# A down projection in Strassen's form: another order of its fourteen units, and of the work on the other engines around them

## The chip, the cores and the metric

The kernel runs on one NeuronCore of a Trainium2 chip. The metric is the device time of one execution in microseconds, as the median of several runs. The engines are called TensorE (matrix products), VectorE, ScalarE, GpSimd (almost unused here) and SyncE, whose queue issues all transfers from device memory.

## The reference, cut to what matters

The program runs two transformer blocks on 256 tokens of width 2048 in fp32. Each block ends with a feed-forward part with a hidden width of 5632. All that the change touches is the last product of these two parts and the work that runs beside it.

```python
# first block (D_MODEL = 2048, FFN_HIDDEN = 5632)
def swiglu(h, w_gate_up, w_down):
    gu = jnp.einsum('bsd,df->bsf', h, w_gate_up)
    gate, up = jnp.split(gu, [FFN_HIDDEN], axis=-1)
    return jnp.einsum('bsf,fd->bsd', jax.nn.silu(gate) * up, w_down)
...
h = h + swiglu(rmsnorm(h, ffn_norm_w[l]), w_gate_up[l], w_down[l])
```

After the first block stand its final norm and the pre-mix norm of the second block, so the tokens are squared, summed and multiplied by gains twice before the second block's first projections read them. The second block's feed-forward multiplies a depthwise convolution and gelu of the gate half with the up half, then multiplies by its own w_down, norms the result (post_ffn_gain) and adds it to the residual.

## The kernel before

**Units.** All weights stream through the core once, in units of 128 x 2048 fp32 (1 MB), in one fixed order. Each unit passes four steps. SyncE loads it into one of four slots of `raw`. ScalarE copies it, rounded to the TensorE format, to `w_hi` (`split`, line 737, semaphore `hi_made`). VectorE writes the remainder `raw - w_hi` to `w_lo` (`split`, line 1288, `lo_made`). TensorE multiplies with the high part (`hi_used`), then with the low part (`lo_used`). Activations are also kept as a high and a low half. `w_hi` and `w_lo` have two buffers each (SPLIT = 2), so the copy of unit u+2 waits until TensorE has read the high part of unit u, and its remainder until the low part is read. Each engine's instructions run in the order in which they are written; the loops over units on ScalarE and VectorE call `split(u + form + 2)` in each step and place their other work before or after it.

**Feed-forward stages.** Each feed-forward part has two groups. A group first computes 22 tiles of hidden values, two units for each (`gated`), and then multiplies them with its share of w_down (`down`). Of a pair of units, VectorE adds the accumulator halves (`total`, line 1300, which also frees the accumulator banks), scales them, and after ScalarE's activation multiplies gate and up; ScalarE copies the result (line 934 in the first, 1211 in the second feed-forward), and VectorE forms its remainder. Of the second feed-forward's last group, ScalarE then loads another function table (`prepare(ACT.Sqrt)`, line 752).

**The down projection.** It runs in two passes, p = 0 (the first) and 1 (the second), of two blocks of 512 output columns each. Of the 22 hidden tiles, the first eight are taken as a 2 x 2 block problem (two k-blocks of four tiles, two column blocks, two blocks of 128 tokens), which Strassen's scheme computes with seven block products instead of eight. A pass has 14 units, called forms: seven products M_1 to M_7 (12 matmuls each: `product`, lines 2338, 2340, 2344) and seven ordinary ones (24 matmuls each: PLAIN_1 to PLAIN_6, `by_tokens`, lines 2319 and 2326, and MIXED, `both_columns`, lines 2369 and 2377, which takes the last two tiles for both column blocks).

The products need sums of weight blocks. VectorE makes four in each pass (`weight_sum(u, n)`, line 1571, 128 x 2048 each):

- sum 1, `B_12 - B_11` into `w_sum`, is the weight of M_5; it waits for both pieces to be loaded
- sum 2, `B_22 - w_sum`, is that of M_6; it can only be made after M_5's remainder, because it overwrites `w_sum`
- sum 3, `B_22 - B_12` in B_12's slot, is that of M_7
- sum 4, `B_21 - w_sum` in B_21's slot, is that of M_4

`WEIGHT_SUMS` makes ScalarE wait for the sum instead of a transfer. The B pieces are loaded once and used for more than one form (`PIECE_OF`), so a pass loads 11 pieces. `PIECES` gives their order, the place in the slot order that each takes, and their content; `FREED_BY[n]` is the form whose remainder must be made before piece n may be loaded; `NEXT_SLOTS` is the slot order that the pass hands on. The first four pieces of a pass wait for the remainders of the four units before it, one each.

Products that feed more than one output block are read out of the accumulator while it goes on: `snap` on VectorE, or `first_out` on ScalarE in the second feed-forward's first group, counted by `snapped`. When a column block is complete, VectorE adds it to the tokens (`added`, line 1529) or to `ff_out` (`out_part`, `out_sum_both`), and frees the two banks.

**Token work behind the last down projection of the first block (g = 1).** For each block n of 512 columns: ScalarE squares the tokens (`v_square`, line 959); TensorE transposes them (`turn_tokens`, eight transposes, line 2434); ScalarE copies them with a gain to `xa`, the next projection's input (`both_high`, line 879, four instructions); VectorE makes the remainders (`tokens_low`, line 1537, four instructions, `op_lo`) and multiplies the tokens by a gain (`final_gain`, line 1667, two instructions, `h_read`); ScalarE squares these (`x_square`, line 966, two squares, each waiting for one of the two gains). Blocks 0 and 2 are handled at the end of the first and of the second pass, block 1 in the middle of the second pass, block 3 after the passes. The next projection (`first_two`, line 2293) takes its first 12 matmuls from blocks 0 to 2 and waits for `op_lo` of each tile.

## Time and profile before

| | |
|---|---|
| median of 3 runs | 2660.02 us (2659.88 to 2660.03) |
| the profiled execution | 2660.03 us, of which its instructions span 2658.2 us |
| TensorE busy | 2637.8 us, 99% of the span, 13950 matmuls |
| VectorE busy | 1854.8 us, 70% |
| ScalarE busy | 1303.6 us, 49% |
| GpSimd busy | 3.5 us |
| transfers | 497.23 MB, 53% of the queues' capacity in time |
| chain of work that ended last | TensorE 92%, VectorE 4%, transfers 2%, ScalarE 1% |
| mean granted TensorE clock | 0.999 |

Busy time is what an engine spent in its instructions. For TensorE the ends of matmuls are modelled, so its waits are best read from the distance between starts. "Idle before <-" behind an instruction names what ended the wait ahead of it.

### The profile page before, as it was taken

The numbers are of one execution on the slowest core, as the hardware profiler recorded it, in microseconds if no ns is written. First come the engines' busy times: TensorE is split into PE (matmuls) and PEld (weight loads), VectorE is DVE, ScalarE is ACT, GpSimd is POOL, SyncE is SP. The second block draws the span as 40 slices with busy tenths as digits, with TensorE's granted clock in tenths as the row PEclk, the third lists the DMA queues.
The fourth block names the chain that finished last, engine by engine and source line by source line (L and its number), as shares of the span: only waits on it lengthen the run. The fifth ranks groups of instructions, "written<-read, shape, count | busy, mean of one in ns | idle before, by whom it ended". The sixth has DMA issues, their size and how long they took to land.

```text
span 2658.2 us, 37139 instructions
## 1 busy us (share of the span) xinstructions
PE 2637.8 (99%) x13950; PEld 2271.1 (85%) x13950; DVE 1854.8 (70%) x1881; ACT 1303.6 (49%) x1313; POOL 3.5 (0%) x8
## 2 busy tenths in 40 slices
PE   9999999999999999999999999999999999999998
PEld 8888888888888888888888888888888888888876
DVE  7646666665555556875557878888777787677878
ACT  6544444444445444544444566645554455444454
POOL 0000000000000000000000000000000000000000
PEclk9999999999999999999999999999999999999999
DMA  7555555455555555465555554543545545555554
GB/s 251 190 190 175 174 189 184 166 203 190 206 193 183 194 189 193 173 226 191 187 188 186 183 207 170 171 157 130 206 174 189 189 164 200 207 188 189 189 206 142
DMA packets 71871, 497.23 MB, mean 187 GB/s; under 512 B 8183, under 2 KB 9432, under 8 KB 12648
## 3 DMA queue, kind: packets, MB, share of 16 engines
q1 hardware_dynamic: 71784, 496.06, 53.1%
q8 instruction: 56, 0.92, 0.1%
q14 instruction: 31, 0.25, 0.0%
HBM read 493.93 MB, written 2.10 MB: 187 GB/s over the span
## 4 chain that ended last, share of the span: by engine, by line
PE 92%; DVE 4%; DMA 2%; ACT 1%; issue 1%; SPq 0%; DVEq 0%; ACTq 0%
PE acc L2263 37%; PE acc L2271 19%; PE acc L2319 10%; PE acc L2499 7%; PE acc L2326 5%; PE acc L2504 3%; DVE w_lo L1288 2%; PE acc L2344 1%; PE acc L2369 1%; PE acc L2340 1%; PE acc L2338 1%; ACT w_hi L737 1%; DMA raw<-in_w_down 1%; PE acc L2626 1%; PE acc L2293 1%
## 5 line engine op out<-in xcount | busy, mean ns | idle before, releaser
L1288 DVE TENSOR_TENSOR w_lo<-raw,w_hi 128x2048 fp32r<-128x2048 f32 (+1 forms) x467 | 1063.6, 2280 | 344.7 <-ACT w_hi L737 318.8
L737 ACT ACTIVATE w_hi<-raw 128x2048 fp32r<-128x2048 f32 (+1 forms) x467 | 889.6, 1906 | 773.9 <-PE acc L2263 334.8
L2263 PE MATMUL acc<-xa,w_hi 128*128 128x512 f32 x4480 | 1071.3, 391 | 0.0
L2263 PEld LDWEIGHTS acc<-xa,w_hi 128*128 128x128 f32 x4480 | 824.3, 188 | 161.4 <-issue 0.7
L2271 PEld LDWEIGHTS acc<-xa,w_lo 128*128 128x128 f32 x4480 | 574.2, 191 | 23.6 <-DVE w_lo L1288 2.0
L2271 PE MATMUL acc<-xa,w_lo 128*128 128x256 f32 x4480 | 581.6, 283 | 1.2 <-DVE w_lo L1288 1.2
L1300 DVE TENSOR_TENSOR tmp<-acc,small 128x512 f32<-128x512 f32 x120 | 83.0, 691 | 243.3 <-ACT small L747 242.8
L2319 PE MATMUL acc<-w_hi,hid 128*128 128x512 f32 x768 | 183.2, 390 | 1.8 <-ACT w_hi L737 1.7
L2499 PE MATMUL acc<-w_hi,xa 128*128 128x512 f32 x768 | 182.4, 390 | 0.0
L2319 PEld LDWEIGHTS acc<-w_hi,hid 128*128 128x128 f32 x768 | 143.4, 188 | 32.9 <-ACT w_hi L737 3.5
L2499 PEld LDWEIGHTS acc<-w_hi,xa 128*128 128x128 f32 x768 | 143.8, 188 | 29.7
L2326 PE MATMUL acc<-w_lo,hid 128*128 128x512 f32 x384 | 95.2, 389 | 0.0
L2504 PE MATMUL acc<-w_lo,xa 128*128 128x512 f32 x384 | 94.9, 389 | 0.0
L1206 ACT ACTIVATE tmp<-tmp 128x256 f32<-128x256 f32 x44 | 18.4, 418 | 155.5 <-DVE tmp L2132 155.5
L2326 PEld LDWEIGHTS acc<-w_lo,hid 128*128 128x128 f32 x384 | 72.1, 188 | 15.0
L2504 PEld LDWEIGHTS acc<-w_lo,xa 128*128 128x128 f32 x384 | 72.1, 188 | 15.0
L747 ACT ACTIVATE small<-acc 128x512 f32<-128x512 f32 x120 | 71.7, 598 | 10.9
L934 ACT ACTIVATE hid<-tmp 128x256 f32 (+1 forms) x44 | 18.4, 418 | 104.1 <-DVE tmp L1640 104.1
L2319 PE MATMUL acc<-w_hi,xb 128*128 128x512 f32 x256 | 61.1, 391 | 0.0
L2319 PEld LDWEIGHTS acc<-w_hi,xb 128*128 128x128 f32 x256 | 47.8, 188 | 9.8
L931 ACT ACTIVATE tmp<-tmp 128x256 f32<-128x256 f32 x44 | 18.4, 419 | 71.5 <-DVE tmp L1634 71.5
L2338 PE MATMUL acc<-w_hi,hid 128*128 128x512 f32 x128 | 50.2, 392 | 1.6 <-ACT w_hi L737 1.6
(379 smaller groups left out, 2093.3 us busy)
## 6 DMA issues: line engine op xcount, KB each, us to landing
raw<-in_w_in SPq DMA_DIRECT2D x158, 1024.0 KB, 4.9
raw<-in_w_gate_up SPq DMA_DIRECT2D x88, 1024.0 KB, 4.9
raw<-in_w_down SPq DMA_DIRECT2D x88, 1024.0 KB, 4.9
raw<-in_w_up SPq DMA_DIRECT2D x87, 1024.0 KB, 4.9
raw<-in_w_out SPq DMA_DIRECT2D x32, 1024.0 KB, 4.9
raw<-in_w_uq SPq DMA_DIRECT2D x3, 1024.0 KB, 5.0
h_tok<-in_x_tok SPq DMA_DIRECT2D x1, 2048.0 KB, 9.2
raw<-in_w_ukv SPq DMA_DIRECT2D x4, 512.0 KB, 3.5
```

What stands on the lines that cost most here:

```text
L737: act.activation(hi_part(u, run)[:, 0:kt * P], raw_of(u)[:, 0:kt * P], ACT.Copy).then_inc(hi_made, splits(u, run))
L747: act.activation(small[:], acc[:, b:b + 2, S:2 * S], ACT.Copy).then_inc(small_made, 2)
L1288: dve.tensor_tensor(lo_part(u, run)[:, 0:kt * P], raw_of(u)[:, 0:kt * P], hi_part(u, run)[:, 0:kt * P], ALU.subtract).then_inc(lo_made, sp ...
L1300: dve.tensor_tensor(tmp[:, 0:2], acc[:, b:b + 2, 0:S], small[:], ALU.add).then_inc(acc_free, 2)
L2263: last = pe.matmul(acc[:, bnk], w_hi[:, u % SPLIT, k * P:(k + 1) * P], x[:, k0 + k], start=first and k == 0, stop=False)
L2271: last = pe.matmul(acc[:, bnk, S:2 * S], w_lo[:, u % SPLIT, k * P:(k + 1) * P], x[:, k0 + k, 0:S], start=False, stop=final and k == kt - 1)
L2293: last = pe.matmul(acc[:, bank(t + j)], w_hi[:, (u + j) % SPLIT, k * P:(k + 1) * P], x[:, k], start=(k == 0), stop=False)
L2319: last = pe.matmul(acc[:, bank(t + c)], a, w, start=(first and k == 0 and half == 0), stop=False, skip_group_check=more)
L2326: last = pe.matmul(acc[:, bank(t + c)], x[:, k0 + k, c * P:(c + 1) * P], lo_part(u, 0)[:, k * 512:(k + 1) * 512], start=False, stop=(final ...
L2338: pe.matmul(acc[:, bank(t)], x_hi(k), w, start=(first and k == 0), stop=False, skip_group_check=more)
L2499: last = pe.matmul(acc[:, bank(t + c)], x, w, start=(m == 0 and k == 0 and half == 0), stop=False)
L2504: last = pe.matmul(acc[:, bank(t + c)], xa[:, 4 * m + k, c * P:(c + 1) * P], w_lo[:, u % SPLIT, k * DV:(k + 1) * DV], start=False, stop=(m ...
```

## The change

The fourteen forms of a pass get another order. Before: PLAIN_1, PLAIN_2, M_1, M_5, M_2, PLAIN_3, M_6, M_3, M_7, MIXED, PLAIN_4, M_4, PLAIN_5, PLAIN_6. After: PLAIN_1, M_1, M_5, M_2, PLAIN_2, M_6, M_3, M_7, PLAIN_3, M_4, MIXED, PLAIN_4, PLAIN_5, PLAIN_6. The pieces, their slots and what frees them follow: B_11, B_22 and B_12 are now the second, third and fourth of a pass (before: third, fourth, fifth). The four weight sums, the readouts, the column additions and the token work take other places in the loops. Sum 1 of a first pass stands ahead of the last pair's `total` (before: behind its second `split`); sum 1 of a second pass moves from PLAIN_6 to PLAIN_5; sum 2 stands behind the `split` of M_5 (before: of M_2); sum 4 behind the `split` of PLAIN_3. `tokens_low`, `final_gain`, `both_high` and `x_square` of block 2p move from PLAIN_5 to PLAIN_6. In the second feed-forward the weight sums and column sums change alike; there ScalarE's `first_out` calls go behind `split`, `out_square(1)` to PLAIN_2 and VectorE's `out_gain(1)` to PLAIN_3. The matmuls are the same in number and shape, as are all other instructions. `split` loses two lines that add a constant loop offset to the unit's number.

```diff
-PLAIN_1, PLAIN_2, M_1, M_5, M_2, PLAIN_3, M_6, M_3, M_7, MIXED, PLAIN_4, M_4, PLAIN_5, PLAIN_6 = range(FORMS)
+PLAIN_1, M_1, M_5, M_2, PLAIN_2, M_6, M_3, M_7, PLAIN_3, M_4, MIXED, PLAIN_4, PLAIN_5, PLAIN_6 = range(FORMS)
...
-B_11, B_22, B_12, B_21 = 2, 3, 4, 5
+B_11, B_22, B_12, B_21 = 1, 2, 3, 4
...
-FREED_BY = (None, None, None, None, PLAIN_1, PLAIN_2, M_1, PLAIN_3, M_3, M_7, M_4)
-NEXT_SLOTS = (2, 3, 0, 1)
+FREED_BY = (None, None, None, None, PLAIN_1, M_1, PLAIN_2, M_3, M_7, PLAIN_3, M_4)
+NEXT_SLOTS = (2, 3, 1, 0)
...
@@ SyncE, down_loads
-                    if n == 6:
+                    if n == 5:
                         sp.wait_ge(w_summed, sums_before(u) + 1)
...
@@ ScalarE, first feed-forward
                     for form in range(FORMS):
-                        if g and form == PLAIN_5:
+                        split(u + form + 2)
+                        if g and p and form == PLAIN_2:
+                            v_square(1)
+                        if g and p and form == PLAIN_3:
+                            both_high(1)
+                        if g and p and form == MIXED:
+                            x_square(1)
+                        if g and form == PLAIN_4:
                             v_square(2 * p)
-                        split(u + form + 2)
-                        if g and p and form == M_7:
-                            v_square(1)
-                        if g and p and form == MIXED:
-                            both_high(1)
-                            x_square(1)
-                        if g and form == PLAIN_5:
+                        if g and form == PLAIN_6:
                             both_high(2 * p)
                             x_square(2 * p)
...
@@ VectorE, gated (both feed-forwards)
                         if p or ahead < 1:
                             split(u + 2, run)
+                        if last and p:
+                            weight_sum(u0 + 2 * GT, 1)
                         total(t, run, 2)
...
                         if p or ahead < 2:
                             split(u + 3, run)
-                        if last and p:
-                            weight_sum(u0 + 2 * GT, 1)
...
@@ VectorE, first feed-forward, over the forms
-                        if form == M_7:
-                            weight_sum(u, 4)
-                        if form == M_4:
-                            added(2 * p, u, M_4)
+                        if form == MIXED:
+                            added(2 * p, u, MIXED)
                         if form == PLAIN_6:
                             added(2 * p + 1, u, PLAIN_6)
                         split(u + form + 2)
-                        if form == M_1:
+                        if form == PLAIN_1:
                             weight_sum(u, 2)
...
                         if form == M_2:
                             weight_sum(u, 3)
-                        if form == PLAIN_6 and p + 1 < PASSES:
+                        if form == M_3:
+                            weight_sum(u, 4)
+                        if form == PLAIN_5 and p + 1 < PASSES:
                             weight_sum(u + FORMS, 1)
-                        if g and p and form == MIXED:
+                        if g and p and form == PLAIN_3:
                             tokens_low(1, DT, V_LAT, gain)
+                        if g and p and form == M_4:
                             final_gain(1)
-                        if g and form == PLAIN_5:
+                        if g and form == PLAIN_6:
                             tokens_low(2 * p, DT, V_LAT, gain)
                             final_gain(2 * p)
...
@@ TensorE, down
                 plain(PLAIN_1, b_11, 8, first=True)
-                plain(PLAIN_2, b_11, 12)
                 pe.wait_ge(acc_free, b_22 + 1)
                 product(u + M_1, b_22, *hidden(0, 0), first=True, final=True)
                 pe.wait_ge(x_sums_lo, 3 * (group + 1))
                 product(u + M_5, b_12, *sums_14(1), first=True, final=True)
                 product(u + M_2, b_11, *hidden(4, 0))
-                plain(PLAIN_3, b_11, 16)
+                plain(PLAIN_2, b_11, 12)
...
                 product(u + M_7, b_22, *hidden(0, 1), final=True, more=True)
+                plain(PLAIN_3, b_11, 16)
+                product(u + M_4, b_21, *hidden(4, 1))
                 if p == 0:
                     pe.wait_ge(op_lo, v1 + GT)
-                both_columns(u + MIXED, t, snaps + 4)
-                if after:
-                    after(MIXED)
+                pe.wait_ge(snapped, snaps + 4)
+                both_columns(u + MIXED, t)
                 plain(PLAIN_4, b_12, 8)
-                product(u + M_4, b_21, *hidden(4, 1), final=True)
```

## Rows read from the trace of the kernel before

**Rows 1.** Waits of TensorE: what it waited for, us in total, times, longest.
```profile
PE acc L2319 <- ACT w_hi L737: 1.7, 3, 0.9
PE acc L2344 <- DVE w_lo L1288: 1.6, 6, 0.6
PE acc L2338 <- ACT w_hi L737: 1.6, 1, 1.6
```

**Rows 2.** Timeline of TensorE, PLAIN_4, M_4, PLAIN_5: start, us, instruction.
```profile
1122.55 3.79 PE L2319 MATMUL acc<-w_hi,hid 128*128 128x512 f32 x16
...
1127.99 0.39 PE L2338 MATMUL acc<-w_hi,hid 128*128 128x512 f32 x1
...
1130.71 0.62 PE L2319 MATMUL acc<-w_hi,hid 128*128 128x512 f32 x2
```

**Rows 3.** Windows over the four down stages: PE, PEld, DVE, ACT, POOL, clock, DMA.
```profile
1083.19:1199.43 116.24, 115.33 (x506) 94.06 (x505) 91.19 (x54) 54.42 (x32) 0.00 (x0) 1.00 0.55 201
1444.34:1563.51 119.17, 118.03 (x530) 96.55 (x529) 99.44 (x72) 65.49 (x67) 0.00 (x0) 1.00 0.55 201
2167.98:2284.66 116.68, 115.99 (x507) 94.06 (x505) 87.88 (x49) 58.36 (x40) 0.00 (x0) 1.00 0.55 201
2530.43:2637.85 107.42, 105.02 (x458) 84.89 (x457) 89.15 (x57) 53.48 (x40) 0.00 (x0) 1.00 0.50 185
```

**Rows 4.** Timeline of TensorE: one group of token transposes and what follows.
```profile
1567.66 1.04 PE L2434 MATMUL aux<-ident,h_tok 128*128 128x128 f32 x8
1568.46 2.08 PE L2293 MATMUL acc<-xa,w_hi 128*128 128x512 f32 x8
```

**Rows 5.** Timeline, first feed-forward, group 0: SyncE, VectorE, ScalarE around the first PLAIN_1.
```profile
1076.68 5.33 SPq L620 DMA_DIRECT2D raw<-in_w_down  x2
...
1079.36 2.29 DVE L1288 TENSOR_TENSOR w_lo<-raw,w_hi 128x2048 fp32r<-128x2048 f32 x1 [1.38 <-ACT w_hi L737]
1084.16 0.69 DVE L1300 TENSOR_TENSOR tmp<-acc,small 128x512 f32<-128x512 f32 x1 [2.51 <-ACT small L747]
...
1085.50 2.28 DVE L1288 TENSOR_TENSOR w_lo<-raw,w_hi 128x2048 fp32r<-128x2048 f32 x1
1087.70 2.28 DVE L1571 TENSOR_TENSOR w_sum<-raw 128x2048 f32<-128x2048 f32 x1
...
1090.76 1.90 ACT L737 ACTIVATE w_hi<-raw 128x2048 fp32r<-128x2048 f32 x1
```

**Rows 6.** Timeline at the start of the second pass, group 0.
```profile
1141.59 0.62 PE L2319 MATMUL acc<-w_hi,hid 128*128 128x512 f32 x2
...
1143.29 2.29 DVE L1288 TENSOR_TENSOR w_lo<-raw,w_hi 128x2048 fp32r<-128x2048 f32 x1 [0.22 <-DVE h_tok L1529]
...
1145.46 1.92 ACT L737 ACTIVATE w_hi<-raw 128x2048 fp32r<-128x2048 f32 x1 [3.52 <-PE acc L2319]
```

**Rows 7.** The page's DMA issues: count, KB each, us to landing.
```profile
raw<-in_w_down SPq DMA_DIRECT2D x88, 1024.0 KB, 4.9
```

**Rows 8.** Timeline before the down projection of both groups of the second feed-forward.
```profile
2177.05 1.90 ACT L737 ACTIVATE w_hi<-raw 128x2048 fp32r<-128x2048 f32 x1
...
2525.78 0.33 SPq L620 DMA_DIRECT2D raw<-in_w_down  x1
...
2531.41 0.69 DVE L1300 TENSOR_TENSOR tmp<-acc,small 128x512 f32<-128x512 f32 x1 [2.12 <-ACT small L747]
...
2541.01 1.89 ACT L737 ACTIVATE w_hi<-raw 128x2048 fp32r<-128x2048 f32 x1
```

**Rows 9.** Timeline of VectorE and ScalarE, first feed-forward, group 1, end of the first pass.
```profile
1500.13 1.65 DVE L1537 SCALAR_TENSOR_TENSOR xa<-aux,both_gain,xa 128x256 fp32r<-128x256 f32 x4
1501.70 1.28 DVE L1667 TENSOR_TENSOR h_tok<-h_tok,first_row 128x512 f32<-128x512 f32 x2
...
1502.41 0.63 ACT L966 ACTIVATE squares<-h_tok 128x512 f32<-128x512 f32 x1 [2.88 <-DVE h_tok L1667]
...
1503.85 1.90 ACT L737 ACTIVATE w_hi<-raw 128x2048 fp32r<-128x2048 f32 x1
```

More of the change, by code:

```diff
@@ L1240, in _ @@
                     for form in range(FORMS):
+                        split(u + form + 2)
+                        if g == 0 and form == M_5:
+                            first_out(u, t, 3, M_1, 2 * p, 0)
+                            first_out(u, t, 2, M_5, 2 * p + 1, 1)
                         if g == 0 and form == M_6:
@@ L1244, in _ @@
                             first_out(u, t, 3, M_7, 2 * p, 1)
-                        split(u + form + 2)
-                        if g == 0 and form == M_5:
-                            first_out(u, t, 3, M_1, 2 * p, 0)
-                            first_out(u, t, 2, M_5, 2 * p + 1, 1)
                         if g == 0 and form == PLAIN_6 and p == 0:
@@ L2124, in gated @@
                             split(u + 2, run)
+                        if last and p:
+                            weight_sum(u0 + 2 * GT, 1)
                         total(t, run, 2)
@@ L2156, in out_sum @@
                     else:
-                        dve.wait_ge(lo_used, u1 + FORMS * (c // 2) + (PLAIN_6 if c % 2 else M_4) + 1)
+                        dve.wait_ge(lo_used, u1 + FORMS * (c // 2) + (PLAIN_6 if c % 2 else MIXED) + 1)
                     dve.wait_ge(snapped, 4 * len(PASS_STARTS) - 8 + 4 * (c // 2) + 4)
@@ L2208, in _ @@
                             snap(u, b_22, M_7, ff_out[:, 2 * p, 1])
-                        if form == M_7:
-                            weight_sum(u, 4)
-                        if form == M_4:
+                        if form == MIXED:
                             if g:
@@ L2214, in _ @@
                             else:
-                                out_part(2 * p, u, M_4)
+                                out_part(2 * p, u, MIXED)
                         if form == PLAIN_6:
@@ L2221, in _ @@
                         split(u + form + 2)
-                        if form == M_1:
+                        if form == PLAIN_1:
                             weight_sum(u, 2)
@@ L2228, in _ @@
                             weight_sum(u, 3)
-                        if form == PLAIN_6 and p + 1 < PASSES:
+                        if form == M_3:
+                            weight_sum(u, 4)
+                        if form == PLAIN_5 and p + 1 < PASSES:
                             weight_sum(u + FORMS, 1)
-                        if g and p and form == MIXED:
+                        if g and p and form == PLAIN_3:
                             out_gain(1, 0)
@@ L2594, in after @@
                     def after(form):
-                        if g and p and form == MIXED:
+                        if g and p and form == PLAIN_3:
                             turn_tokens(1, 4 * COLS, V_LAT)
```

21 lines of the change are left out of this document (6 added, 15 removed), and 14 rows, old and new, of the table PIECES.

## The prediction

> **What bounds the kernel now.** I read the page first (its table stands above): TensorE is busy for 99% of the span. The change removes and adds no matmul, so only TensorE's idle time can move. TensorE's own waits [rows 1] are short and sit on the lines of the down projections, which the change reorders: it waits there for ScalarE's rounding copy (L737) or VectorE's remainder (L1288) of a weight piece.
>
> To size them I set the length of the down stages against their matmuls. A plain form (24 matmuls) takes 1127.99 - 1122.55 = 5.44 us and a product (12 matmuls) 1130.71 - 1127.99 = 2.72 us when nothing waits [rows 2]. A pass has seven forms of 24 (MIXED is one) and seven products: 7 x 5.44 + 7 x 2.72 = 57.12 us. The four down stages, which I call A and B (first feed-forward, groups 0 and 1), C and D (second), last [rows 3]:
>
> - A: 116.24, less 2 x 57.12 = 2.00 us of waiting
> - B: 119.17, less 114.24 and less three token transposes of 1568.46 - 1567.66 = 0.80 us each [rows 4] = 2.53
> - C: 116.68, 2.44 us
> - D up to its PLAIN_5: 107.42, less 114.24 - 10.88 = 103.36: 4.06
>
> Together 11.0 us. That is the most the change can win (0.4%), and it shows why only the order of work around each form matters.
>
> **How a form is fed.** With two buffers, ScalarE copies form f+2 once TensorE has read the high half of form f, and VectorE subtracts once the copy is done and f's low half is used. Subtractions back to back start 2.20 us apart (1085.50, 1087.70 [rows 5]); a weight sum costs the same. A product leaves 2.72 us, so VectorE has 0.52 us to spare per product and a weight sum ahead of a product's subtraction costs up to 2.20 us.
>
> **Part 1: weight sum 2 moves ahead of M_2's subtraction.** Before, VectorE did M_2's subtraction and then sum 2. Now the loop does M_5's subtraction, sum 2, M_2's subtraction. If M_5's subtraction starts at x after the start T of PLAIN_1, M_2's ends at x + 2 x 2.20 + 2.29. TensorE wants it after 5.44 + 2.72 + 2.72 + 8 x 0.227 = T + 12.70. With 0.06 us of hand-over the limit is x = 5.95.
>
> In a second pass ScalarE starts the third form's copy at 1145.46 - 1141.59 = T + 3.87 [rows 6], so x = 3.87 + 1.92 + 0.03 = 5.82: no wait, by 0.1 us. The pass start in B is the exception (part 4).
>
> In the first passes of A and B the feed-forward's tail is in the way. Weight sum 1 now runs before the last pair's total (L1300). In A PLAIN_1's subtraction starts at 1079.36, so the sum fits from 1081.6 to 1083.9, inside the idle time ahead of 1084.16 [rows 5]: free, if its piece is there. That piece (B_12) is now the fourth of the pass and is asked for in the place of 1076.68 [rows 5]; with 4.9 us to landing [rows 7] it is there at 1081.6: in time. Without this cover it costs up to 2.2. So the hidden copy and then the copy of the third form come 2.20 us earlier: 1090.76 - 2.20 = 1088.56, ready 1090.46; x = 1090.49 - 1083.19 = 7.30. M_2's low half waits 7.30 - 5.95 = 1.35 us. A wait costs more than its length, since the first matmuls behind it come slower: the profile names 4.9 us in ten waits [rows 1] where the stages' lengths give 11.0. Part of that is the overlap of a modelled 0.39 us matmul with a distance of 0.227, which ready times don't have; for the restart I take 0.2 us a wait (an estimate, from 0 to 0.4). So 1.55 each in A and B; bounds 0.5 (if VectorE is reached 1 us sooner) and 2.2.
>
> **Part 2: weight sum 4 moves ahead of M_4.** M_4's piece is the sum, and M_4 now comes right behind PLAIN_3. From the end of M_3's high half: ScalarE starts PLAIN_3's copy 0.24 later (3.87 less 16 x 0.227 [rows 6]), 1.92 long; then the subtraction 2.20, sum 4 2.28, M_4's copy 1.92, its subtraction 2.29, with hand-overs of 0.03 to 0.06 in between: 11.03. TensorE arrives after 0.91 + 2.72 + 5.44 + 1.81 = 10.88. A wait of 0.15, with restart 0.3, in seven of eight passes (B's second has transposes of 0.80 in between that hide it): 2.1 us. Bounds 0 and 0.5 each.
>
> **Part 3: C and D, first pass.** The second feed-forward's tail has the longer gate chain. The fourth piece is asked for at 2525.78 in D [rows 8]; with 4.9 us it lands at 2530.68, although VectorE is free before that. Weight sum 1 then ends its slot at 2532.88, and the total behind it, at 2531.41 before, starts 1.47 late: a new wait for a DMA. All that VectorE does next shifts by that; M_1 comes one form earlier and its low half waits about 0.3. The hidden copy shifts by +1.47 - 2.20, so the third form's copy (behind the table load) starts at 2541.01 - 0.73 = 2540.28 and ends at 2542.17. Before, the third form began at T + 10.88; now, M_5, at T + 8.16 = 2538.59. x = 2542.20 - 2530.43 = 11.77, so M_2's low half comes 11.77 - 5.95 = 5.82 us late in all; with restarts of three waits 6.1. In C, which has no table load there, the copy moves by as much, from 2177.05 to 2176.32 (I take D's shift, since the order is the same); it is ready at 2178.22, x = 2178.25 - 2167.98 = 10.27: 4.3, with restarts 4.6. If the piece landed in time these would be 1.5 less each; if landing took 6 us, 1.1 more.
>
> **Part 4: B's second pass, and the seam behind B.** At PLAIN_6 instead of PLAIN_5 stand now VectorE's four token remainders (L1537) and two gain products (L1667), and ScalarE's squares (L966) of these products. Before, this ran while TensorE was in PLAIN_6 [rows 9]. Now it runs after the column is added up at the end of PLAIN_6 and after M_1's subtraction, which starts at T + 1143.29 - 1141.59 = 1.70 [rows 6]. So the remainders start at T + 3.91, the products at +1.57 = 5.48 (1501.70 - 1500.13), the squares 0.71 later at 6.19, and the copy that is queued behind them on ScalarE (M_5's) 1.44 later (1503.85 - 1502.41) at 7.63, not 3.87. x = 7.63 + 1.92 + 0.03 = 9.58: M_2 is 3.63 us late, 3.9 with restarts.
>
> At the end of B's second pass the same group prepares column block 2 (tiles 8 to 11) of the next projection's input, which its first 12 matmuls read. The last remainder starts at 3.91 + 3 x 0.39 = 5.08 and ends 0.47 later, at 5.55, after the projection's start; TensorE wants it at 11 x 0.227 = 2.50. So 3.1 us. Behind it ScalarE's further squares and copies delay the third unit's copy to about 13.6 + 1.9 = 15.5 where TensorE, itself 3.2 late, arrives at 15.2: 0.3 more, with restarts 3.8 in all. Bounds 2.5 and 4.5.
>
> **What is covered.** The other pieces' landing, out_square and out_gain moved in D, first_out moved in C, v_square(1) and both_high(1): each falls where ScalarE or VectorE is 1 us or more ahead, mostly behind the plain forms. They cost nothing; uncovered, 0.6 to 1.6 us each. PLAIN_3's old waits for its copy (up to 0.9 us [rows 1]) are gone: the form behind M_2 now has its piece asked for at M_1's subtraction, two products and more ahead.
>
> **Sum.** Waits after: A 1.55 + 2 x 0.3 = 2.15; B 1.55 + 0.3 + 3.9 + 3.8 = 9.55; C 4.6 + 0.6 = 5.2; D 6.1 + 0.6 = 6.7. Together 23.6, against 11.0: +12.6 us. On the profiled execution, 2660.03 us (span 2658.2 and 1.8 around it), this gives 2672.6; its time is within 0.01 of the median, so I predict 2672.6.
>
> **A rule that could make it longer.** Every down stage has a granted clock of 1.00, the higher level of 2.4 GHz, also D with its waits of up to 1.6 us [rows 1, 3]. D's new wait for M_5 is some 3.2 us at once. If the clock fell to 1.2 GHz in it, a product's 2.72 us would become 5.44: 2.7 us more, perhaps twice, 2675 to 2678. The Trainium skill, "TensorE: Matmul & The Clock Gate", section "HAM oscillation — how this bites in real kernels", says that TensorE left waiting long enough between groups of matmuls is put back to its lower clock. By the rule the time would be the higher one; no row here shows it.
>
> **Rivals.**
> - Faster. M_5's subtraction starts before T + 5.95 in every pass, so sum 2 is hidden and only M_4's waits stay: 2660 - 11 + 2 = 2651. For it: second passes do so by 0.1 us and the old waits (up to 1.6 us [rows 1]) go. Against it: x is 7.3, 10.3 and 11.8 in the first passes by rows that the change hardly moves. It decides at x = 5.95 there and at the seams of part 4. 0.05.
> - No change. Parts 1 to 3 as forecast but smaller, or part 4 and the late piece absent together: 2672.6 - 7.7 - 3.0 = 2661.9. 0.08.
> - Only part 4 absent, because the queues reach the token work sooner than I think: 2672.6 - 7.7 = 2664.9. 0.08, half of it on either side of the bound below.
> - The piece lands in time in C and D: 2672.6 - 3.0 = 2669.6. 0.07.
> - The clock falls in D: 2675 to 2678. 0.03.
> - Longer for another reason (slower landing, a wait that I don't see): 2676 to 2680. 0.07.
> - The sum as above, 2669 to 2676: 0.62.
>
> A measurement of this kernel tells about 0.2% (5.3 us) from no change. Faster 0.05, same 0.12, slower 0.83. The range reaches from just below the third rival to the middle of the last two: 2664 to 2678.
>
> **What would show it.** TensorE waiting for VectorE ahead of M_2's low half (L2344) in the first passes, for ScalarE ahead of M_5 in C, D and B's second pass, for VectorE's L1537 in the projection behind B; VectorE waiting for a transfer ahead of its first weight sum (L1571) in C and D; second passes of A and C of 57.4 us. The forecast fails if the first passes show no such waits, above all if the copies of M_5 start with PLAIN_1's high half and not with the gate's tail.

## The result, and the profile after

The changed kernel takes 2675.6 us (median of 4 runs, 2674.2 to 2677.02); the kernel before, measured beside it, 2659.95 (4 runs, 2657.81 to 2660.03). The ratio is 1.006, 95% interval 1.0045 to 1.0075: slower by 15.7 us, where 12.6 were predicted. The profiled execution took 2673.37 us, 1.8 of it around a span of 2671.6; it is the fastest of the seven executions of this kernel on record here (up to 2677.02). Names and lines are those of the changed kernel: the copy that rounds a weight piece is L735, its remainder L1285, a weight sum L1568, the total L1297, the token remainders L1534, plain forms L2317 and L2324, the high half of a product L2336 and L2338 and its low half L2342.

First the waits of TensorE in the changed kernel (what it waited for, us in total, times, longest), which answer to [rows 1]:

```profile
PE acc L2342 <- DVE w_lo L1285: 7.0, 9, 1.5
PE acc L2336 <- ACT w_hi L735: 6.0, 3, 3.1
PE acc L2291 <- DVE xa L1534: 2.5, 1, 2.5
```

The waits ahead of plain forms are gone. Instead the low halves of products wait for a remainder (nine times), three products wait for their copy, and the projection behind B waits for the token remainders. All three kinds are the ones forecast.

Next the windows over the down stages of the changed kernel, which answer to [rows 3]: from each start to its end the length, the busy time (with instructions) of PE, PEld, DVE, ACT and POOL, the granted clock, the DMA share and GB/s. In order: A's first and second pass, B's first and second, the stretch behind B up to L2261, C, and D up to its PLAIN_5.

```profile
1083.42:1142.49 59.07, 57.71 (x254) 47.15 (x253) 46.88 (x29) 27.97 (x18) 0.00 (x0) 1.00 0.57 202
1142.49:1200.08 57.59, 57.59 (x254) 47.14 (x252) 43.17 (x25) 26.47 (x15) 0.00 (x0) 1.00 0.56 201
1444.98:1504.92 59.94, 58.64 (x263) 47.98 (x261) 46.85 (x29) 29.32 (x22) 0.00 (x0) 1.00 0.57 206
1504.92:1567.74 62.82, 59.81 (x270) 48.72 (x268) 48.69 (x37) 34.88 (x39) 0.00 (x0) 1.00 0.52 189
1567.74:1583.35 15.61, 12.93 (x74) 10.62 (x72) 9.32 (x16) 9.54 (x23) 0.00 (x0) 1.00 0.22 80
2175.38:2295.14 119.76, 117.45 (x506) 95.34 (x505) 88.45 (x49) 58.37 (x40) 0.00 (x0) 0.99 0.55 197
...
2540.89:2651.26 110.37, 105.34 (x458) 85.05 (x457) 90.72 (x59) 54.95 (x40) 0.00 (x0) 1.00 0.50 180
```

The stretch behind B in the kernel before, in the same view:

```profile
1563.51:1575.54 12.03, 12.03 (x74) 10.69 (x73) 7.52 (x10) 9.32 (x17) 0.00 (x0) 1.00 0.35 127
```

Less the matmuls as the prediction counts them (57.12 a pass, 0.80 for the transposes in B's first pass and 1.60 in its second, 103.36 in D) this leaves:

| stage | waiting before | forecast after | measured after |
|---|---|---|---|
| A, first and second pass | 2.00 together | 1.85, 0.3 | 1.95, 0.47 |
| B, first and second pass | 2.53 together | 1.85, 3.9 | 2.02, 4.10 |
| behind B | 0 | 3.8 | 15.61 - 12.03 = 3.58 |
| C | 2.44 | 5.2 | 5.52 |
| D up to PLAIN_5 | 4.06 | 6.7 | 7.01 |
| together | 11.0 | 23.6 | 24.65 |

The difference of the last row to 11.0 is 13.6 us; the two profiled executions differ by 2673.37 - 2660.03 = 13.3. Some 0.08 us of each pass's "waiting" is rounding: 252 matmuls at 0.227 us are 57.20, not 57.12.

**A's first pass.** Timeline of VectorE and ScalarE in the changed kernel (start, length, engine, instruction, in brackets the idle time before it and what ended it), which answers to [rows 5]; under it TensorE's matmul that waited:

```profile
1081.88 2.29 DVE L1568 TENSOR_TENSOR w_sum<-raw 128x2048 f32<-128x2048 f32 x1
1084.39 0.69 DVE L1297 TENSOR_TENSOR tmp<-acc,small 128x512 f32<-128x512 f32 x1 [0.23 <-ACT small L745]
...
1088.80 1.90 ACT L735 ACTIVATE w_hi<-w_sum 128x2048 fp32r<-128x2048 f32 x1
...
1090.78 2.29 DVE L1285 TENSOR_TENSOR w_lo<-w_sum,w_hi 128x2048 fp32r<-128x2048 f32 x1 [1.44 <-ACT w_hi L735]
1093.11 2.29 DVE L1568 TENSOR_TENSOR w_sum<-raw,w_sum 128x2048 f32<-128x2048 f32 x1
1095.32 2.28 DVE L1285 TENSOR_TENSOR w_lo<-raw,w_hi 128x2048 fp32r<-128x2048 f32 x1
...
1095.91 0.39 PE L2338 MATMUL acc<-w_hi,hid 128*128 128x512 f32 x1
1097.66 1.20 PE L2342 MATMUL acc<-w_lo,hid 128*128 128x512 f32 x4 [1.36 <-DVE w_lo L1285]
```

Weight sum 1 has its piece in time, and the total waits 0.23 us for ScalarE instead of 2.51: the sum lies in idle time. M_5's remainder starts at x = 1090.78 - 1083.42 = 7.36 (forecast 7.30), sum 2 starts 1093.11 - 1090.78 = 2.33 behind it (the prediction took 2.20), and M_2's remainder ends at 1097.60, 0.06 before TensorE goes on. The matmul stands 1097.66 - 1095.91 = 1.75 behind the one before it, instead of 0.227: a wait of 1.52, of which the profile names 1.36.

**B's second pass and behind it**, the same view of the changed kernel:

```profile
1506.62 2.29 DVE L1285 TENSOR_TENSOR w_lo<-raw,w_hi 128x2048 fp32r<-128x2048 f32 x1 [0.21 <-DVE h_tok L1526]
1508.83 1.65 DVE L1534 SCALAR_TENSOR_TENSOR xa<-aux,both_gain,xa 128x256 fp32r<-128x256 f32 x4
1510.40 1.28 DVE L1664 TENSOR_TENSOR h_tok<-h_tok,first_row 128x512 f32<-128x512 f32 x2
...
1512.56 1.89 ACT L735 ACTIVATE w_hi<-w_sum 128x2048 fp32r<-128x2048 f32 x1
...
1514.59 0.47 PE L2336 MATMUL acc<-w_hi,s_hi 128*128 128x512 f32 x1 [1.35 <-ACT w_hi L735]
...
1521.36 1.19 PE L2342 MATMUL acc<-w_lo,hid 128*128 128x512 f32 x4 [1.47 <-DVE w_lo L1285]
...
1572.18 1.67 PE L2291 MATMUL acc<-xa,w_hi 128*128 128x512 f32 x4 [2.47 <-DVE xa L1534]
```

Token remainders, gain products and M_5's copy start at T + 3.91, T + 5.48 and T + 7.64 (T = 1504.92), each within 0.01 of the forecast. Most of the lateness comes in two waits, M_5 for its copy and M_2 for its remainder, and then once more behind B.

**D**, the same view of the changed kernel, which answers to [rows 8]:

```profile
2536.25 3.86 SPq L620 DMA_DIRECT2D raw<-in_w_down  x2
...
2541.26 2.29 DVE L1568 TENSOR_TENSOR w_sum<-raw 128x2048 f32<-128x2048 f32 x1 [1.51 <-DMA raw<-in_w_down]
2543.47 0.68 DVE L1297 TENSOR_TENSOR tmp<-acc,small 128x512 f32<-128x512 f32 x1
...
2549.46 1.28 ACT L750 ACT_TABLE_LOAD   x1
...
2550.86 1.89 ACT L735 ACTIVATE w_hi<-w_sum 128x2048 fp32r<-128x2048 f32 x1
...
2552.79 2.29 DVE L1285 TENSOR_TENSOR w_lo<-w_sum,w_hi 128x2048 fp32r<-128x2048 f32 x1 [2.89 <-ACT w_hi L735]
...
2552.90 0.47 PE L2336 MATMUL acc<-w_hi,s_hi 128*128 128x512 f32 x1 [3.08 <-ACT w_hi L735]
```

The first transfer of 2536.25 is the sum's piece; it lands 4.9 us later and VectorE stands idle 1.51 us for it (C: 1.59). The total behind it starts at T + 2.58, and TensorE waits 3.08 us at once for M_5's copy, the longest wait of the kernel.

**The clock.** Before, the granted clock was 1.00 in every down stage. In the profiled execution of the changed kernel it fell once in these stages, as M_5's wait in C ended. A window and TensorE's timeline there:

```profile
2186.00:2189.00 3.00, 3.00 (x7) 2.41 (x8) 2.97 (x2) 1.61 (x1) 0.00 (x0) 0.50 0.43 180
```

```profile
2185.95 0.77 PE L2336 MATMUL acc<-w_hi,s_hi 128*128 128x512 f32 x1 [1.56 <-ACT w_hi L735]
2186.52 0.63 PE L2338 MATMUL acc<-w_hi,s_lo 128*128 128x512 f32 x1
2186.95 0.63 PE L2336 MATMUL acc<-w_hi,s_hi 128*128 128x512 f32 x1
...
2192.72 1.19 PE L2342 MATMUL acc<-w_lo,hid 128*128 128x512 f32 x4 [0.38 <-DVE w_lo L1285]
```

A clock of 0.50 is the lower level, 1.2 GHz; matmuls stand 0.43 us apart instead of 0.227. Yet C is only 0.3 longer than forecast: M_2's low half, which waits up to 1.5 us where the clock holds (the first view), waits 0.38 here. VectorE's remainder decides the end either way, and the slow matmuls fill time that would have been waited.

### The profile page after: what moved, and what is told of

It reads as the page before. It is cut to its first block, busy times and chain, and to the rows that moved or that the text cites. A ratio compares the mean times of both kernels' runs of the same rounds, so it can differ in the third digit from the quotient of the medians.

```text
span 2671.6 us, 37118 instructions
## 1 busy us (share of the span) xinstructions
PE 2640.9 (99%) x13950; PEld 2272.8 (85%) x13950; DVE 1856.3 (69%) x1881; ACT 1303.7 (49%) x1313; POOL 3.5 (0%) x8
## 4 chain that ended last, share of the span: by engine, by line
PE 93%; DVE 4%; ACT 1%; issue 1%; DMA 1%; DVEq 0%; SPq 0%; ACTq 0%
PE acc L2261 37%; PE acc L2269 19%; PE acc L2317 10%; PE acc L2493 7%; PE acc L2324 5%; PE acc L2498 3%; PE acc L2342 2%; DVE w_lo L1285 2%; PE acc L2338 2%; PE acc L2336 2%; PE acc L2365 1%; ACT w_hi L735 1%; PE acc L2620 1%; PE acc L2372 1%; PE aux L2761 1%
## 5 line engine op out<-in xcount | busy, mean ns | idle before, releaser
L1285 DVE TENSOR_TENSOR w_lo<-raw,w_hi 128x2048 fp32r<-128x2048 f32 (+1 forms) x467 | 1063.0, 2280 | 342.7 <-ACT w_hi L735 315.4
L735 ACT ACTIVATE w_hi<-raw 128x2048 fp32r<-128x2048 f32 (+1 forms) x467 | 889.4, 1906 | 801.6 <-PE acc L2261 337.2
L2261 PE MATMUL acc<-xa,w_hi 128*128 128x512 f32 x4480 | 1071.4, 391 | 0.2 <-ACT w_hi L735 0.2
L2261 PEld LDWEIGHTS acc<-xa,w_hi 128*128 128x128 f32 x4480 | 824.3, 188 | 161.8 <-issue 1.1
L2269 PEld LDWEIGHTS acc<-xa,w_lo 128*128 128x128 f32 x4480 | 574.1, 191 | 23.6 <-DVE w_lo L1285 2.0
L1297 DVE TENSOR_TENSOR tmp<-acc,small 128x512 f32<-128x512 f32 x120 | 82.9, 691 | 234.9 <-ACT small L745 234.4
L2317 PE MATMUL acc<-w_hi,hid 128*128 128x512 f32 x768 | 182.6, 390 | 0.0
L2317 PEld LDWEIGHTS acc<-w_hi,hid 128*128 128x128 f32 x768 | 143.8, 188 | 29.8
L2324 PE MATMUL acc<-w_lo,hid 128*128 128x512 f32 x384 | 95.2, 389 | 0.0
L2324 PEld LDWEIGHTS acc<-w_lo,hid 128*128 128x128 f32 x384 | 72.1, 188 | 15.0
L745 ACT ACTIVATE small<-acc 128x512 f32<-128x512 f32 x120 | 71.7, 598 | 10.9
L2317 PE MATMUL acc<-w_hi,xb 128*128 128x512 f32 x256 | 61.1, 391 | 0.0
L2317 PEld LDWEIGHTS acc<-w_hi,xb 128*128 128x128 f32 x256 | 47.8, 188 | 9.8
L2336 PE MATMUL acc<-w_hi,hid 128*128 128x512 f32 x128 | 49.9, 390 | 0.0
```

Of the source, the lines that this page charges most:

```text
L735: act.activation(hi_part(u, run)[:, 0:kt * P], raw_of(u)[:, 0:kt * P], ACT.Copy).then_inc(hi_made, splits(u, run))
L745: act.activation(small[:], acc[:, b:b + 2, S:2 * S], ACT.Copy).then_inc(small_made, 2)
L1285: dve.tensor_tensor(lo_part(u, run)[:, 0:kt * P], raw_of(u)[:, 0:kt * P], hi_part(u, run)[:, 0:kt * P], ALU.subtract).then_inc(lo_made, sp ...
L1297: dve.tensor_tensor(tmp[:, 0:2], acc[:, b:b + 2, 0:S], small[:], ALU.add).then_inc(acc_free, 2)
L2261: last = pe.matmul(acc[:, bnk], w_hi[:, u % SPLIT, k * P:(k + 1) * P], x[:, k0 + k], start=first and k == 0, stop=False)
L2269: last = pe.matmul(acc[:, bnk, S:2 * S], w_lo[:, u % SPLIT, k * P:(k + 1) * P], x[:, k0 + k, 0:S], start=False, stop=final and k == kt - 1)
```

## The experiments

Ten more runs were made, one of them of the changed kernel again. They were made in three groups, each on another chip and with the kernel before beside it: 2659.42 us beside tokens_back, sum2_back, sum4_early and sum1_back, 2659.66 beside before_tokens_late, three, placed and after_again, 2660.0 beside pieces_swapped and copy_early. Below, a difference to "the changed kernel" or to after_again is one of medians, and most of them are between groups. A second reading is given where it matters, by the excess of each over the kernel before beside it, which is 15.7 us for the changed kernel and 15.5 for after_again.

The 95% intervals of the ratios of sum2_back, sum4_early, sum1_back and pieces_swapped overlap that of the changed kernel. The single times are farther apart: all eleven of the changed kernel lie between 2673.37 and 2677.02, and of these four runs only sum4_early reaches in among them, with 2673.74.

**tokens_back: the token work at its old place,** PLAIN_5, on VectorE ahead of weight sum 1; everything else of the change is kept.

```diff
-                        if g and form == PLAIN_6:
+                        if g and form == PLAIN_5:
                             both_high(2 * p)
                             x_square(2 * p)
...
-                        if g and form == PLAIN_6:
+                        if g and form == PLAIN_5:
                             tokens_low(2 * p, DT, V_LAT, gain)
                             final_gain(2 * p)
```

> The changed kernel, with the token work of column blocks 0 and 2 back at PLAIN_5, ahead of weight sum 1, on ScalarE and VectorE. Theory (the late token work holds up M_5's copy in B's second pass, 3.9 us, and the first matmuls behind B, 3.8 us): 7.7 us less than the changed kernel, about 2668; in the trace TensorE no longer waits at L2291 for VectorE's remainder, and stage B's second pass loses its waits ahead of M_5 and M_2. Rival (the seams were bound by TensorE's own order of forms and the transposes, the token work only shows up as the last of several things): less than 2 us.

Measured: 2667.38 us (2666.35 to 2668.29), ratio 1.003 (1.0019 to 1.004), 8.2 less than the changed kernel; its excess over the kernel before beside it is 8.0, so 7.7 less. The window over B's second pass in its profile:

```profile
1504.80:1563.89 59.09, 59.09 (x270) 48.89 (x268) 49.92 (x38) 35.12 (x40) 0.00 (x0) 1.00 0.56 202
```

59.09 us against 62.82: the pass has 59.09 - 58.72 = 0.37 of waiting left. The wait behind B is gone, and the stretch there takes 12.02 us as in the kernel before (12.03). Part 4 is some 8 us, the largest part of the slowdown.

**before_tokens_late: the same move alone, in the kernel before.** Its order of forms and its sums stay; the token work goes from PLAIN_5 to PLAIN_6.

```diff
-                        if g and form == PLAIN_5:
+                        if g and form == PLAIN_6:
                             both_high(2 * p)
                             x_square(2 * p)
...
-                        if g and form == PLAIN_5:
+                        if g and form == PLAIN_6:
                             tokens_low(2 * p, DT, V_LAT, gain)
                             final_gain(2 * p)
```

> The kernel before, with one part of the change alone: the token work of column blocks 0 and 2 moved from PLAIN_5 to PLAIN_6 on ScalarE and VectorE. Theory (the place of the token work costs by itself, whatever the order of the forms): 3.8 us at the projection behind B, and 1.5 to 2 us ahead of M_1 in B's second pass, where a plain form more stands in front: 5.5 us more than before, about 2665.5. Rival (it costs only together with the new order of forms): within 1 us of before.

Measured: 2666.83 us (2665.35 to 2668.84), ratio 1.0027 (1.0017 to 1.0037): 7.2 more than the kernel before beside it, where 5.5 were expected. Waits of TensorE in its profile:

```profile
PE acc L2319 <- ACT w_hi L737: 3.1, 5, 1.6
PE acc L2293 <- DVE xa L1537: 2.5, 1, 2.5
```

The wait of 2.5 us in the projection behind B is the same as in the changed kernel. The move costs 7 us with the old order of forms too, so it is the place in the queues and not the order of the forms that costs. Stage B is 2.5 us longer than before (121.70 against 119.17) and the stretch behind it 4.5 (16.51 against 12.03); there the clock fell in this profile, which the expectation did not count.

**sum2_back: weight sum 2 behind M_2's remainder again.**

```diff
-                        if form == PLAIN_1:
+                        if form == M_1:
                             weight_sum(u, 2)
```

> The changed kernel, with weight sum 2 back behind M_2's subtraction. Theory (the sum ahead of M_2's subtraction delays it by 2.2 us): the waits at M_2's low half go, 1.5 to 1.7 us each in the first passes of A, B, D and B's second, less in C, together about 7.5 us; but all that VectorE does after it is 0.45 late at M_3's low half, about 0.5 us in each of eight passes. Net 3 to 4 us less, about 2672. Rival (a sum costs VectorE its 2.2 us wherever it stands, the wait only moves): within 1 us of the changed kernel.

Measured: 2672.03 us (2671.37 to 2673.32), ratio 1.0049 (1.0032 to 1.0066), 3.6 less. Waits of TensorE in its profile:

```profile
PE acc L2336 <- ACT w_hi L735: 6.0, 3, 3.1
PE acc L2342 <- DVE w_lo L1285: 3.3, 13, 0.5
```

M_2's waits of 1.5 us are gone, those of M_5 are the same as in the changed kernel (6.0 in 3), and more small ones of up to 0.5 come in. Sum 2 ahead of M_2 is worth 3 to 4 us (3.0 by the excess over the kernel before); what remains of the lateness ahead of M_2 sits in M_5's copy.

**sum4_early: weight sum 4 ahead of PLAIN_3's remainder.** The loop makes both in its step M_3; only their order is turned round.

```diff
+                        if form == M_3:
+                            weight_sum(u, 4)
                         split(u + form + 2)
...
-                        if form == M_3:
-                            weight_sum(u, 4)
```

> The changed kernel, with weight sum 4 ahead of PLAIN_3's subtraction, in the time in which VectorE waits for PLAIN_3's copy. Theory (sum 4 between PLAIN_3's and M_4's subtraction makes M_4's low half late by 0.15 us, with restart 0.3, in seven passes): 2.1 us less, about 2673.5, and no wait ahead of M_4. Rival (the wait ahead of M_4 is set by ScalarE's copy, not by the sum): no change.

Measured: 2672.46 us (2671.38 to 2673.74), ratio 1.0048 (1.0031 to 1.0064): 3.1 less than the changed kernel's 2675.6 and 2.7 less than its second measurement (after_again, below), against 2.1 forecast; by the excess over the kernel before, 2.6 and 2.4. The times alone leave the size open; the profile settles it. Its window over A's second pass, where M_4's low half is the only late one in the changed kernel:

```profile
1141.82:1199.08 57.26, 57.26 (x254) 47.22 (x253) 43.16 (x25) 26.59 (x15) 0.00 (x0) 1.00 0.56 201
```

57.26 us against 57.59 is 0.33 less, and A's first pass loses 59.07 - 58.81 = 0.26. At M_4 TensorE has no distance over 0.23 left (1176.18 to 1176.41). So the part is worth about 0.3 us a pass, as forecast, 2.1 in seven; the rest of what the times show is the scatter between executions. Its rival, that ScalarE's copy sets the wait, falls.

**sum1_back: weight sum 1 behind the last pair's total again.** This undoes what the prediction called free.

```diff
-                        if last and p:
-                            weight_sum(u0 + 2 * GT, 1)
                         total(t, run, 2)
...
                             split(u + 3, run)
+                        if last and p:
+                            weight_sum(u0 + 2 * GT, 1)
                         dve.wait_ge(gate_out, pairs + (g0 + 1 + p))
```

> The changed kernel, with weight sum 1 of the first passes back behind the last pair's second split. Theory (its early place takes 2.2 us off the gate's tail in A and B for nothing, and in C and D 2.2 less 1.5 that it waits for its piece): M_5's copy comes 2.2 us later in A and B, 0.7 later in C and D, while M_1's wait of 0.4 goes there: 5 us more, about 2680.6. Rival (in C and D the wait for the piece is the cost, so the old place is better there, and A and B have room for it): 2 to 3 us less, about 2673.

Measured: 2680.4 us (2679.77 to 2681.58), ratio 1.0078 (1.0061 to 1.0095), 4.8 more. TensorE waits 10.9 us in five waits for L735, the longest 4.3. The early place of sum 1 is the one part of the change that wins time, given the new order of forms: with M_5 as the third form, a sum at the end of the gate's tail delays it.

**three: tokens_back, sum2_back and sum4_early together.** What is left of the change is the order of forms and of loads, and sum 1's place.

> The changed kernel with three parts placed otherwise: token work back at PLAIN_5, sum 2 behind M_2's subtraction, sum 4 ahead of PLAIN_3's. Theory (the new order of forms costs nothing by itself, the places of the other work do): left are the waits ahead of M_5 in C and D (3 and 4 us) and 0.5 us ahead of M_3 in each pass, 11 us as before: 2659 to 2661. Rival (the new order of forms is itself worse, three products standing close behind the pass start): 2665 or more.

Measured: 2662.11 us (2660.95 to 2664.6), ratio 1.0011 (1.0002 to 1.002). The three differences of 8.2, 3.6 and 3.1 add to 14.9, and 13.5 came; by the excess over the kernel before beside each, 7.7, 3.0 and 2.6 add to 13.3, and 13.2 came. So the parts add up. With the queue orders put back, the new order of forms is 2.45 us slower than the old (0.02 to 0.2%). That is 1.1 above the expected range: TensorE still waits 4.6 us for M_5's copies in C and D, and in this profile the clock fell behind the wait in D.

**after_again: the changed kernel once more.**

> The changed kernel once more, on the same chip as the others. Theory of the 2 to 3 us by which its median exceeds the sum of waits (the granted clock falls to half behind the 1.7 to 3.2 us waits of C and D in some executions, more often than in the one profiled): 2674 to 2677, and a profiled clock mean of 0.997 to 0.999 with one or two stretches at half clock behind M_5's wait. Rival (the excess is in the launch or the transfers): a clock mean as in the kernel before.

Measured: 2675.13 us (2673.44 to 2676.47), ratio 1.0058 (1.0043 to 1.0074). The profiled execution took 2675.55, 2.2 more than the first. Windows of it: the stretch behind B, D and a part of D, and last a part of the stretch behind B.

```profile
1567.37:1584.23 16.86, 14.39 (x73) 12.19 (x72) 10.27 (x16) 10.60 (x23) 0.00 (x0) 0.90 0.21 74
...
2542.82:2653.48 110.66, 107.18 (x459) 87.08 (x457) 90.72 (x59) 54.94 (x40) 0.00 (x0) 0.97 0.50 180
2555.00:2558.00 3.00, 3.00 (x7) 2.40 (x8) 2.97 (x2) 1.60 (x1) 0.00 (x0) 0.50 0.00 0
```

```profile
1574.00:1577.00 3.00, 3.00 (x16) 3.00 (x16) 0.13 (x1) 2.73 (x10) 0.00 (x0) 0.50 0.51 213
```

The clock fell three times in this execution: behind the wait of 2.47 us behind B, in C, and behind the 3.08 us in D. Behind B the stretch is 16.86 - 15.61 = 1.25 us longer; in D only 110.66 - 110.37 = 0.3, since M_2's low half then waits for nothing. Another 1.2 us come from TensorE's wait for L2050 between B and C, where no fall is and the change does nothing. That wait is 0.6 to 0.8 us in six of the twelve profiles (the kernel before and placed among them) and 1.5 to 1.6 in the other six, so two single profiles can differ by 1 us for this alone; what makes it longer was not tried.

**pieces_swapped: B_12 is loaded ahead of B_22.** The piece of weight sum 1 is asked for one place earlier; nothing else moves.

```diff
     (1, ((0, 0), (1, 0), (2, 0), (3, 0))),
-    (2, ((4, 1), (5, 1), (6, 1), (7, 1))),
-    (3, ((0, 1), (1, 1), (2, 1), (3, 1))),
+    (2, ((0, 1), (1, 1), (2, 1), (3, 1))),
+    (3, ((4, 1), (5, 1), (6, 1), (7, 1))),
...
-B_11, B_22, B_12, B_21 = 1, 2, 3, 4
+B_11, B_12, B_22, B_21 = 1, 2, 3, 4
...
-NEXT_SLOTS = (2, 3, 1, 0)
+NEXT_SLOTS = (3, 2, 1, 0)
```

> The changed kernel, in which only B_12 and B_22 change places in the order of loads, so that the piece of weight sum 1 is asked for one place earlier. Theory: in C and D the first weight sum no longer waits 1.5 to 1.6 us for its transfer, so the total, the gate and M_5's copy come that much earlier and the waits of M_5 and M_2 in C and D shrink by 1.5 us each stage: 3 us less than the changed kernel, about 2672.5. Rival: the gate chain on ScalarE is as late without the transfer's wait, the transfer was hidden: within 1 us of the changed kernel's 2675.4.

Measured: 2671.1 us (2669.77 to 2672.01), ratio 1.0043 (1.0026 to 1.006), 4.0 less than after_again where 3 were expected. Windows over C and D in its profile:

```profile
2175.16:2293.22 118.06, 115.86 (x507) 94.13 (x505) 87.13 (x49) 58.36 (x40) 0.00 (x0) 1.00 0.56 199
2538.98:2647.67 108.69, 106.27 (x459) 86.35 (x457) 89.47 (x59) 54.92 (x40) 0.00 (x0) 0.98 0.50 183
```

C and D are each 1.7 us shorter (119.76 and 110.37 in the changed kernel). VectorE no longer waits for a transfer ahead of sum 1. The rival, that the transfer was hidden, falls.

**copy_early: M_5's copy leaves the end of ScalarE's queue.** It moves ahead of the last hidden tile's copy, its remainder on VectorE ahead of that tile's remainder (which moves behind the remainder that the loop makes at M_1), and D's table load behind PLAIN_2. The lines below are those of the first feed-forward and of the table load.

```diff
                         act.activation(tmp[:, 2], tmp[:, 0], ACT.Silu).then_inc(gate_out, 1)
+                        if last and p:
+                            split(u + 4, run)
...
+                        if last and p:
+                            split(u + 4, run)
+                            return
                         dve.wait_ge(op_hi, pairs + (v0 + 1 + p))
                         dve.tensor_tensor(hid[:, m, S:2 * S], tmp[:, 3], hid[:, m, 0:S], ALU.subtract).then_inc(op_lo, 1)
...
-                if g:
-                    prepare(ACT.Sqrt)
...
+                        if g and p == 0 and form == PLAIN_2:
+                            prepare(ACT.Sqrt)
```

> The changed kernel, in which only the copy of M_5 on ScalarE moves ahead of the last hidden tile's copy (and its subtraction on VectorE ahead of that tile's remainder), and D's table load moves behind PLAIN_2. Theory: M_2's waits of 1.5 us in A and B go, and in C and D what is left is the transfer's 1.5 us or less, so 1.5 + 1.5 + 2.8 + 4.6 = 10.4 us at most and 8 at least are won: 2665 to 2667.5. Rival: the end of the gate itself (not its place in the queue) sets M_5's copy, so little is won: 2671 or more.

Measured: 2665.16 us (2663.19 to 2666.91, 10 runs), ratio 1.0018 (1.0009 to 1.0028), 10.0 less than after_again. Windows over A, C and D in its profile:

```profile
1084.28:1199.49 115.21, 115.21 (x506) 94.32 (x505) 89.82 (x54) 54.44 (x32) 0.00 (x0) 1.00 0.57 204
2175.71:2292.90 117.19, 115.62 (x507) 94.21 (x505) 88.19 (x49) 58.26 (x40) 0.00 (x0) 1.00 0.56 201
2538.66:2644.82 106.16, 104.76 (x459) 85.22 (x457) 90.50 (x59) 54.97 (x40) 0.00 (x0) 1.00 0.51 188
```

A is 1.45 us shorter than in the changed kernel, C 2.6 and D 4.2. What made M_5's copy late was mostly its place in the queue behind the last hidden tile. D gains 1.6 more than C, about the 1.28 of the table load, but the load was not moved alone. The rival falls. The 1.5 us of the late transfer are still in C and D here.

**placed: the new order of forms, with a place for each piece of work.** It is copy_early, pieces_swapped, sum4_early and tokens_back together.

> The changed order of forms with all other work put where the theory says that it is free: token work at PLAIN_5, sum 4 ahead of PLAIN_3's subtraction, M_5's copy ahead of the last hidden tile's copy on ScalarE and its subtraction ahead of that tile's remainder on VectorE, B_12 loaded before B_22, ScalarE's table load of D moved to PLAIN_2. Theory: M_5's copy starts at T + 3.87 in all passes, the waits left are 0.5 us ahead of M_2 in C and D: about 1.5 us in the four stages instead of 11.0: 2650 to 2652, faster than both kernels. Rival (restart costs and clock falls take the rest): 2655 or more.

Measured: 2652.25 us (2650.85 to 2653.9), ratio 0.9973 (0.9962 to 0.9983): faster than both kernels. Its timeline around the first PLAIN_1, and its windows over A, C and D:

```profile
1087.02 1.92 ACT L737 ACTIVATE w_hi<-w_sum 128x2048 fp32r<-128x2048 f32 x1 [1.06 <-PE acc L2347]
1088.84 0.40 ACT L936 ACTIVATE hid<-tmp 128x256 fp32r<-128x256 f32 x1
...
1088.98 2.29 DVE L1293 TENSOR_TENSOR w_lo<-w_sum,w_hi 128x2048 fp32r<-128x2048 f32 x1 [0.93 <-ACT w_hi L737]
```

```profile
1083.12:1197.73 114.61, 114.61 (x506) 94.45 (x505) 89.83 (x54) 54.69 (x32) 0.00 (x0) 1.00 0.58 205
2164.00:2279.03 115.03, 114.70 (x506) 94.44 (x505) 86.78 (x49) 58.60 (x40) 0.00 (x0) 1.00 0.58 205
2524.79:2629.01 104.22, 103.89 (x458) 85.44 (x457) 89.30 (x59) 55.32 (x40) 0.00 (x0) 1.00 0.52 191
```

M_5's remainder starts at x = 1088.98 - 1083.12 = 5.86 in A, and M_2's low half is 0.07 us late (1095.91, 0.30 behind the matmul before it): sum 2 stands ahead of M_2 and costs next to nothing. In C and D x is 6.34, and M_2's low half is 0.49 late. A, C and D have 0.4, 0.8 and 0.9 us of waiting left, out of 2.4, 5.5 and 7.0. The expectation named these 0.5 us and 2650 to 2652 us; the median is 0.25 above. Against after_again the four parts alone gave 10.0, 4.0, 2.7 and 7.8 us, 24.4 in all; together they gave 22.9.

## Why the prediction was right, and what it sized wrong

The changed kernel became slower by the chain that was forecast, in the range that was given. By its own steps:

- **Part 1** (sum 2 ahead of M_2): the wait is shown, and two terms of it were mis-sized. The prediction let sum 2 start 2.20 us behind M_5's remainder; it starts 2.33 behind (in sum2_back M_2's remainder, which doesn't touch `w_sum`, starts 1092.22 - 1090.01 = 2.21 behind). So the limit of x is 5.82 and not 5.95. Both sides bear this out: at 7.36 M_2's low half is 1.52 us late (7.36 - 5.82 = 1.54), at 5.86 (placed, A) 0.07. Behind the wait the four low matmuls take 1.03 us to the next form (1098.69 in the timeline, less 1097.66) instead of 0.91, so a restart costs 0.12, not 0.2. The two errors cancel: 1.52 + 0.12 = 1.64 against 1.55. That the pass as a whole came so near, 1.95 against 1.85, is in part luck. In second passes, which the prediction called free by 0.1 us, x is 5.83, and the four low matmuls take 1.04 us: 0.13 each. That and the rounding lie between the forecast 57.4 us and the measured 57.59. Undoing the part gave 3.6 us.
- **Weight sum 1 as free in A**: shown, by the total's idle time of 0.23 and by sum1_back.
- **Part 2** (sum 4 ahead of M_4): as forecast. M_4's low half is 0.15 us late in A's second pass, with restart 0.27 (forecast 0.3), and sum4_early takes 0.26 to 0.33 a pass away.
- **Part 3** (C and D): the late piece is shown by VectorE's idle time of 1.51 and 1.59 us (1.47 forecast) and by pieces_swapped; its size was given as 3.0 us, and 3.4 came in the two windows. M_5's remainder in D starts at 2552.79, T + 11.90, forecast 11.77; in C at T + 10.46, forecast 10.27.
- **Part 4**: shown by tokens_back and before_tokens_late. In the profiled execution it is 4.10 + 3.58 = 7.68 us of waiting where 7.7 was forecast; tokens_back gave 7.7 to 8.2.
- **The clock**: this is what the sum left out. The prediction gave the fall 0.03 and priced it at 2.7 us a product. It fell in both profiled executions of the changed kernel, once and three times, and in the profile of each of the eight other runs whose kernel has a wait of 2 us or more (the table at the end). The chance was far too low; the price was too high, because most falls lie ahead of a wait for VectorE, which they shorten. Only behind B, where TensorE had the next pieces ready, did a fall cost up to 1.25 us. The measured 2675.6 lies in that rival's stretch, 2675 to 2678, as well as in the sum's, but not by the rival's way: its fall in D cost 0.3. The Trainium skill, "TensorE: Matmul & The Clock Gate", section "HAM oscillation — how this bites in real kernels", says that a stretch of waiting puts TensorE back to its lower clock. By that rule the trace agrees in part: falls came behind waits of 1.56, 2.47 and 3.08 us, but the 2.47 and 3.08 us passed without one in the first profile.

The forecast of 2672.6 us missed the median by 3.0. Against the profiled execution of 2673.37 it is 0.8: 1.05 us more waiting in the stages, less 0.3 elsewhere. The other 2.2 us lie between this execution and the median. The second profile, which is near the median, has them as 1.25 and 0.3 of clock and 1.2 of the wait for L2050, less 0.6 in other stretches. That the other executions are made up in the same way is not shown; their mean granted clock speaks for it, 0.997 to 0.998 in all six others of the first measurement, against 0.999 in the profiled one and in the kernel before.

The rival "faster" named its own condition, x below 5.95 in every first pass and at the seams. placed comes near it, with 5.86 in A, 5.85 in B and 6.34 in C and D, and is faster: 2652.25 us. The rival's 2651 still had M_4's waits in it, which placed hasn't, so the likeness of the two times is in part chance.

## What to carry to other kernels

An order of matmuls and an order of the work that feeds them are two changes; the same new order of forms took 2675 us with one set of places in the queues and 2652 with another. For each product write down when its remainder must start (here T + 5.8) and check every pass against it with start times from the trace, the passes behind a gate or a group's end first, since they start late. A copy whose own input is ready should not stand in a queue behind one that still has to wait for another engine.

## What the runs showed of the hardware

**The clock.** The granted clock fell to 0.50 behind a wait of only 1.56 us (C) in one execution, while in the same execution waits of 2.47 and 3.08 us left it at 1.00; in another all three places had a fall. Counted over the profiles of all runs, by the wait that TensorE had just before (as the profile names it):

| wait | profiles with it | with a fall |
|---|---|---|
| behind B, 2.5 us | 8 | 5 |
| ahead of M_5 in D, 2.1 to 4.3 us | 8 | 7 |
| ahead of M_5 in C, 1.6 to 2.8 us | 7 | 2 |

Behind the other waits of the down stages, of up to 1.6 us, none of the profiles shows a fall, and the kernel before and placed show none there at all. A fall behind B made the stretch 0.65 to 1.25 us longer (15.61 without, 16.26 to 16.86 with it, with the same wait ahead); where VectorE was behind it cost 0.3 or nothing.

**A restart.** Behind a wait the first distance between two matmuls was 0.31 to 0.34 us instead of 0.227 at a clock of 1.00 (D: 2552.90 to 2553.21), and 0.12 us went in all behind M_2's wait in A.

**VectorE.** A subtraction over 128x2048 that takes and overwrites the tile that the remainder before it reads (weight sum 2) started 2.31 to 2.38 us behind it, a remainder of another tile 2.21. Why is not shown.
